# Conditioning sums over partitions in an fp32 two-block model: transposes with VectorE sums against matmuls with a column of ones

## The chip, the cores and the metric

The kernel runs on one core of one Trainium2 chip. The metric is the time of one execution on the device in microseconds, as the median of several runs.

## The reference, cut to what matters

Two blocks of two layers each work on 256 tokens of width 1024, all in fp32. The first block has a gating mixer, an attention mixer and two MLPs. The second block has four SwiGLU layers with a pooling mixer and a convolution mixer between them, and each of its six sublayers is modulated by a conditioning vector `c`:

```python
cond = jax.nn.silu(c)
for i in range(DEPTH):
    mod = (cond @ ada_w[i] + ada_b[i]).reshape(B, N_SUB, N_MOD, D_MODEL)
    shift, scale, gate = mod[:, :, 0], mod[:, :, 1], mod[:, :, 2]
    h = modulate(rms_norm(x, norm_g[i, 0]), shift[:, 0], scale[:, 0])
    x = x + 0.5 * gate[:, 0, None, :] * swiglu(h, ffn_w_in[i, 0], ffn_w_out[i, 0])
    ...
```

`ada_w` is 2 x 1024 x 9216 in fp32. What this document is about is the end of `cond @ ada_w[i]` for `shift` and `scale`.

## The kernel before

The program is written out by hand: one instruction stream for each engine, with semaphores between them. Tokens are two tiles (t = 0, 1) of 128. Weights come in slabs of 128 x 2048 through a ring of three buffers `raw`. Each product of the large layers is made of three fp32r matmuls, so a slab is split: ScalarE writes `w_hi` (L512), VectorE writes `w_lo` = raw - w_hi (L865), and TensorE multiplies w_hi with x_hi, w_lo with x_hi and w_hi with x_lo (L1327 to L1329, issued in the helper `mm`, L1315). Every tile of an up product is 12 such matmuls of 512 columns for each half of the 1024 inputs.

The phases follow one another: gate_in, positions, gate_out, mlp0, qkv, attn, attn_out, mlp1, final1, ffn0, pool, ffn1, ffn2, conv_in, conv_out, ffn3, final2. In an MLP or FFN phase, chunk c runs up products of two slabs into `up_ps`, ScalarE and VectorE make `mid` from them, TensorE turns `mid` by transposes into `tr_ps` (L1396), ScalarE and VectorE split that into hT_hi and hT_lo (L526, L876), and TensorE adds the down product to `acc`. The transposes of chunk c stand behind the down product of chunk c - 1.

`tr_ps` has two PSUM banks of 512 fp32 columns. All uses of it are numbered ("fills"); fill n goes to bank n % 2. TensorE waits in `bank(n)` (L1384) until `tr_read`, the count of fills that have been read, reaches n - 1, and raises `tr_ready` when a fill is complete.

The conditioning product runs beside the layers. VectorE multiplies pieces of `ada_w` with `cond` and adds them up over the eight groups of 128 rows in `ada_acc` (L930, L933), 128 x 9216, so that only the sum over the 128 partitions is missing. For each of the six sublayers ("sub") `modulation` makes that sum for the 16 tiles of shift and scale. On TensorE (L1487 to L1496) it is cut into two halves of eight tiles. Each tile of 128 x 128 is transposed into a quarter of a bank, so a half fills two banks and a sub four (MOD_FILLS = 4). On VectorE (L937 to L954) four sums over the free axis (L944) read 128 x 512 each and write `mod_sum`; then come the add of the bias (L949), the gain (L951) and `mod_ready`.

The places are fixed by the order of the code. In mlp1, the two halves of sub 0 stand behind the two token tiles of the second up slab of chunk 1 (`between`, L1519). In ffn0, ffn1 and ffn2, the halves of the first sub stand inside the up product of chunk 1, one up tile apart (L1657 to L1659). In ffn0 and ffn2 there is a second sub: its half 0 stands ahead of the first down slab and its half 1 behind it, right ahead of the transposes of mid of chunk 1 (L1641 to L1650). On VectorE, `modulation` stands ahead of the ada pieces of chunk 1 in mlp1, ahead of a split for the first sub of an FFN (L1176), and behind the next split for the second (L1184).

The gates, the third part of each sub, are summed over partitions in another way already: two matmuls (L1622) with `ones[:, :]`, 128 x 128, as the weights and 512 columns of `ada_acc` streamed.

Of the kernel before, what the change touches and what calls it, by code (L numbers as in the profile page):

```python
# [17 lines left out]
ALU = mybir.AluOpType  # L18
ACT = mybir.ActivationFunctionType
AX_X = mybir.AxisListType.X  # L20
# [3 lines left out]
P = 128  # L24
D = 1024
KT = D // P
# [7 lines left out]
FILL = 4  # L34
# [34 lines left out]


MODS = {"mlp1": (0,), "ffn0": (1, 2), "ffn1": (3,), "ffn2": (4, 5)}
MOD_FILLS = 2 * KT // FILL
GATES = {"ffn0": (0, 1), "ffn1": (2,), "ffn2": (3, 4), "ffn3": (5,)}
GATE_HALF = {sub: n for subs in GATES.values() for n, sub in enumerate(subs)}
FFN_AT = {"ffn0": 0, "ffn1": 1, "ffn2": 2, "ffn3": 3}
# [84 lines left out]
def build(nc, x, mix_norm_g, mlp_norm_g, final_norm_g, a_w_in, a_ln_g, a_ln_b, a_w_s, a_b_s, a_w_out,  # L160
# [7 lines left out]
    with ctx:  # L168
        def sb(name, shape, dt=F32):
            return ctx.enter_context(nc.sbuf_tensor(name, shape, dt))  # L170
# [9 lines left out]
        ada_acc = sb("ada_acc", [P, ADA_COLS])  # L180
# [9 lines left out]
        ident = flip[:, 1, :]  # L190
        ones = sb("ones", [P, P])
# [4 lines left out]
        msq = sb("msq", [P, TT])  # L196
        rstd = sb("rstd", [P, TT])
        neg_half = sb("neg_half", [P, 1])
        mod_sum = sb("mod_sum", [P, 2 * KT])
        mod = sb("mod", [P, 3, 2 * KT])  # L200
        gain = sb("gain", [P, 3, KT])
        den = sb("den", [P, 2 * HEADS])
# [37 lines left out]
        tr_ps = ctx.enter_context(nc.psum_tensor("tr_ps", [P, 2, 512], F32))  # L240
# [14 lines left out]
        tr_ready, tr_hi, tr_read = sem("tr_ready"), sem("tr_hi"), sem("tr_read")  # L255
# [585 lines left out]
        def _(dve):  # L841
            steps = [0]

            def own(ins):

                ins.then_inc(dve_step, 1)
                steps[0] += 1
                dve.wait_ge(dve_step, steps[0])
# [88 lines left out]
            def modulation(name, sub):  # L937


                layer, s = divmod(sub, 3)  # L940
                fill = mid_fill(at[name], name, 0) + TT + MOD_FILLS * MODS[name].index(sub)
                for q in range(MOD_FILLS):
                    dve.wait_ge(tr_ready, fill + q + 1)
                    nc.vector.tensor_reduce(mod_sum[:, q * FILL:(q + 1) * FILL],  # L944
                                            tr_ps[:, (fill + q) % 2, :].rearrange("p (f n) -> p f n", n=P),
                                            AX_X, ALU.add).then_inc(tr_read, 1)
                dve.wait_ge(tr_read, fill + MOD_FILLS)
                b = adabT[:, layer, s * 3 * KT:s * 3 * KT + 2 * KT]
                own(nc.vector.tensor_tensor(mod[:, s, :], mod_sum[:, :], b, ALU.add))  # L949
                r0 = ROWS["norm"][0] + KT * sub  # L950
                nc.vector.scalar_tensor_tensor(out=gain[:, s, :], in0=mod[:, s, KT:2 * KT], scalar=1.0,  # L951
                                               in1=vecT[:, r0:r0 + KT], op0=ALU.add, op1=ALU.mult)\
                    .then_inc(mod_ready, 1)
                dve.wait_ge(mod_ready, sub + 1)  # L954
# [19 lines left out]
            last = lambda name: at[name].slab - 1  # L974
# [13 lines left out]
            for c in range(4):  # L988
                ahead(g)
                if c == 1:  # L990
                    p = at["positions"]
# [37 lines left out]
            p = at["gate_out"]  # L1029
            for n in range(NORM_FILLS):  # L1030
                t, b = divmod(n, KT // FILL)
# [43 lines left out]
            p = at["qkv"]  # L1075
# [53 lines left out]
            p = at["attn_out"]  # L1129
# [98 lines left out]
            for q in range(POOLS):  # L1228
                dve.wait_ge(tr_read, at["pool"].tr + q + 1)
                k = slice(2 * q, 2 * q + 2)  # L1230
                for f in range(2):
                    n = 2 * q + f
# [13 lines left out]
            p = at["conv_in"]  # L1246
            own(nc.vector.memset(uT[:, :, 0:CONV_W - 1], 0.0))
            g = p.slab
            q = at["conv_out"]
# [60 lines left out]
        def _(pe):  # L1310
# [3 lines left out]
            def mm(dst, a, b, start=False, stop=False):  # L1314
                return nc.tensor.matmul(dst, a, b, start=start, stop=stop, skip_group_check=True)  # L1315
# [68 lines left out]
            def bank(tr, i=None, per=0):  # L1384

                if tr >= 2:
                    pe.wait_ge(tr_read, plus(i, tr - 1, per))
                return tr_ps[:, tr % 2, :]
# [62 lines left out]
            for c in range(1, 4):  # L1451
                up_chunk(g + 2 * c, free=(gelu_done, 2 * (c - 1) + 1, 0))
                if c == 1:
                    p = at["positions"]
# [7 lines left out]
                    for n in range(NG):  # L1462
                        c0 = n * VLEN
                        while c0 < (n + 1) * VLEN:
                            c1 = min((n + 1) * VLEN, (c0 // 512 + 1) * 512)
                            last = mm(acc[0:HEADS, c0 // D, c0 % D:c0 % D + c1 - c0], rel[:, n * HEADS:(n + 1) * HEADS],
                                      mask_sb[:, n, c0 - n * VLEN:c1 - n * VLEN], start=True, stop=True)
# [4 lines left out]
            for t in range(TT):  # L1472
                pe.wait_ge(vn_ready, t + 1)
                for q in range(GROUPS):
                    last = mm(acc[:, t, q * P:(q + 1) * P], ws_T[:, q, :], g_v[:, t, q * P:(q + 1) * P],
                              start=True, stop=True)
                last.then_inc(mix_ready, 1)
            p = at["gate_out"]
            for n in range(NORM_FILLS):
                t, b = divmod(n, KT // FILL)  # L1480
# [6 lines left out]
            def modulation(name, sub, half):  # L1487

                fill = mid_fill(at[name], name, 0) + TT + MOD_FILLS * MODS[name].index(sub)
                pe.wait_ge(ada_step, 8 * ((sub // 3) * ADA_UNITS + 6 * (sub % 3) + 4))  # L1490
                for q in range(half * MOD_FILLS // 2, (half + 1) * MOD_FILLS // 2):
                    dst = bank(fill + q)
                    for f in range(FILL):
                        n = (sub % 3) * 3 * KT + q * FILL + f
                        last = nc.tensor.transpose(dst[:, f * P:(f + 1) * P], ada_acc[:, n * P:(n + 1) * P], ident)  # L1495
                    last.then_inc(tr_ready, 1)  # L1496

            def mlp(name):
# [35 lines left out]
            p = at["qkv"]  # L1534
# [23 lines left out]
            p = at["attn"]  # L1558
# [49 lines left out]
            p = at["attn_out"]  # L1608
# [74 lines left out]
            p = at["pool"]  # L1683

            pe.wait_ge(pool_landed, 16)
            for q in range(POOLS):
                dst = up_ps[:, q // 2, (q % 2) * TOKENS:(q % 2 + 1) * TOKENS]
# [6 lines left out]
            for q in range(POOLS):  # L1694
                dst = bank(p.tr + q)
# [72 lines left out]
```

## Time and profile before

| | before |
|---|---|
| median of 3 runs | 1605.37 us (1604.02 to 1610.68) |
| the profiled execution | 1607.08 us, span 1605.3 us |
| PE matmul busy | 1524.8 us (95%), 7069 instructions |
| PE weight load busy | 1254.0 us (78%) |
| VectorE busy | 1038.2 us (65%), 1110 instructions |
| ScalarE busy | 707.9 us (44%) |
| DMA | 345.83 MB, mean 215 GB/s |
| mean granted TensorE clock | 0.981 |

The profile counts an engine as busy when an instruction is running on it; matmuls are pipelined, so PE (TensorE matmul) being busy doesn't mean that it runs at its peak. PEld is the weight load, which overlaps PE. In a timeline, the duration of a matmul contains its latency; what a stream of matmuls costs is read from the distance of their starts.

### The profile page before, as it was taken

The page shows a single profiled execution, that of the slowest core. Times are in us where ns is not written, and L with a number is a line of the kernel's source. Part 1 is how long each engine was busy: PE and PEld are TensorE (multiplying, and loading weights), DVE is VectorE, ACT ScalarE, POOL GpSimd, SP SyncE. Part 2 cuts the span into 40 slices and gives each one's busy share as a digit, 9 for nine tenths or more (in the row PEclk, how much of TensorE's full clock was granted, in tenths as well). Part 3 has the DMA queues.
Part 4 walks back from the last instruction along what each step waited for, and adds up shares of the span by engine and source line. Part 5 has one row for each costly group of instructions (what it writes and reads, how often), then busy time and mean ns, then how long its engine had stood idle before and what let it go on. Part 6 is the DMA issues. An engine that isn't in the chain of part 4 may idle for free.

```text
span 1605.3 us, 20507 instructions
## 1 busy us (share of the span) xinstructions
PE 1524.8 (95%) x7069; PEld 1254.0 (78%) x7069; DVE 1038.2 (65%) x1110; ACT 707.9 (44%) x831; POOL 22.0 (1%) x63
## 2 busy tenths in 40 slices
PE   5899999999999999799998899998999999999997
PEld 4778888788778888678887788886788878778886
DVE  4748777545548767567887778887645464764444
ACT  5345444543545454444443434444344444454442
POOL 1000000000000000000000000000000000000000
PEclk9999999999999999899999899999999999999999
DMA  8438777557508788558896279886455546445552
GB/s 260 174 126 324 270 269 274 159 173 243 175 12 295 282 287 289 188 183 309 302 311 229 85 256 318 303 313 217 144 184 188 189 140 204 143 158 185 190 190 76
DMA packets 201892, 345.83 MB, mean 215 GB/s; under 512 B 9531, under 2 KB 105027, under 8 KB 201836
## 3 DMA queue, kind: packets, MB, share of 16 engines
q1 hardware_dynamic: 161420, 267.22, 49.5%
q10 hardware_dynamic: 40416, 77.86, 13.9%
q8 instruction: 35, 0.57, 0.1%
q14 instruction: 21, 0.17, 0.0%
HBM read 343.96 MB, written 1.09 MB: 215 GB/s over the span
## 4 chain that ended last, share of the span: by engine, by line
PE 84%; DVE 8%; ACT 3%; DMA 2%; issue 2%; POOL 1%; SPq 0%; POOLq 0%; DVEq 0%; ACTq 0%
PE up_ps L1315 51%; PE acc L1315 28%; DVE w_lo L865 3%; PE tr_ps L1396 2%; DMA ada_raw<-in_ada_w 2%; PE tr_ps L1315 1%; DVE ada_acc L933 1%; ACT w_hi L512 1%; DVE res L971 1%; ACT xn L534 1%; DVE xn L968 1%; PE tr_ps L1581 1%; ACT xn L549 1%; PE tr_ps L1495 1%; POOL rstd L470 1%
## 5 line engine op out<-in xcount | busy, mean ns | idle before, releaser
L865 DVE TENSOR_TENSOR w_lo<-raw,w_hi 128x2048 fp32r<-128x2048 f32 x245 | 561.1, 2291 | 302.4 <-ACT w_hi L512 301.3
L512 ACT ACTIVATE w_hi<-raw 128x2048 fp32r<-128x2048 f32 x245 | 469.5, 1916 | 313.1 <-PE up_ps L1315 256.7
L1315 PE MATMUL up_ps<-w_hi,xT_hi 128*128 128x512 f32 x1264 | 506.0, 400 | 22.8 <-DVE xT_lo L887 16.5
L1315 PE MATMUL up_ps<-w_hi,xT_lo 128*128 128x512 f32 x1264 | 497.5, 394 | 0.0
L1315 PE MATMUL up_ps<-w_lo,xT_hi 128*128 128x512 f32 x1264 | 497.1, 393 | 0.0
L1315 PEld LDWEIGHTS up_ps<-w_hi,xT_hi 128*128 128x128 f32 x1264 | 240.4, 190 | 75.3 <-issue 16.9
L1315 PEld LDWEIGHTS up_ps<-w_hi,xT_lo 128*128 128x128 f32 x1264 | 240.1, 190 | 51.4
L1315 PEld LDWEIGHTS up_ps<-w_lo,xT_hi 128*128 128x128 f32 x1264 | 240.8, 190 | 47.6
L933 DVE SCALAR_TENSOR_TENSOR ada_acc<-ada_raw,cond,ada_acc 128x512 f32 (+1 forms) x252 | 189.3, 751 | 15.7 <-DMA ada_raw<-in_ada_w 8.0
L1315 PE MATMUL acc<-w_hi,hT_hi 128*128 128x512 f32 x624 | 194.3, 393 | 4.8 <-DVE hT_lo L876 4.8
L1315 PE MATMUL acc<-w_hi,hT_lo 128*128 128x512 f32 x624 | 193.0, 391 | 0.0
L1315 PE MATMUL acc<-w_lo,hT_hi 128*128 128x512 f32 x624 | 192.9, 391 | 0.0
L1315 PEld LDWEIGHTS acc<-w_hi,hT_hi 128*128 128x128 f32 x624 | 116.5, 188 | 30.1 <-DVE hT_lo L876 4.0
L526 ACT ACTIVATE hT_hi<-tr_ps 128x256 fp32r<-128x256 f32 (+1 forms) x122 | 47.8, 441 | 207.4 <-PE tr_ps L1396 203.6
L1315 PEld LDWEIGHTS acc<-w_lo,hT_hi 128*128 128x128 f32 x624 | 117.7, 189 | 24.6
L1315 PEld LDWEIGHTS acc<-w_hi,hT_lo 128*128 128x128 f32 x624 | 117.5, 188 | 24.5
L876 DVE TENSOR_TENSOR hT_lo<-tr_ps,hT_hi 128x256 fp32r<-128x256 f32 (+1 forms) x122 | 55.4, 494 | 75.7 <-ACT hT_hi L526 75.4
L752 ACT ACTIVATE pre<-up_ps 128x256 f32<-128x256 f32 x88 | 33.9, 385 | 134.4 <-PE up_ps L1315 134.3
L534 ACT ACTIVATE xn<-res 128x1024 f32<-128x1024 f32 x24 | 25.7, 1072 | 78.6 <-DVE res L971 70.0
L1167 DVE TENSOR_TENSOR mid<-pre,up_ps 128x256 f32<-128x256 f32 x88 | 34.9, 416 | 22.8 <-ACT pre L752 22.8
L1396 PE MATMUL tr_ps<-flip,xn 128*128 128x128 f32 x160 | 26.4, 318 | 20.1 <-DVE xn L880 15.9
L1396 PEld LDWEIGHTS tr_ps<-flip,mid 128*128 128x128 f32 x304 | 36.6, 140 | 11.2 <-issue 4.2
(121 smaller groups left out, 788.6 us busy)
## 6 DMA issues: line engine op xcount, KB each, us to landing
raw<-in_ffn_w_in SPq DMA_DIRECT2D x176, 512.0 KB, 4.7
ada_raw<-in_ada_w ACTq DMA_DIRECT2D x72, 1024.0 KB, 6.9
raw<-in_ffn_w_out SPq DMA_DIRECT2D x88, 512.0 KB, 4.4
raw<-in_w_up SPq DMA_DIRECT2D x64, 512.0 KB, 4.7
raw<-in_w_down SPq DMA_DIRECT2D x64, 512.0 KB, 4.6
raw<-in_b_w_qkv SPq DMA_DIRECT2D x36, 512.0 KB, 4.4
raw<-in_conv_w_in SPq DMA_DIRECT2D x24, 512.0 KB, 4.6
raw<-in_a_w_in SPq DMA_DIRECT2D x16, 512.0 KB, 6.3
```

Source lines behind the costliest of these rows:

```text
L470: nc.gpsimd.tensor_tensor(dst, src, neg_half[:, 0:1], ALU.pow).then_inc(ready, 1)
L512: nc.scalar.activation(w_hi[:, slot, :], raw[:, slot, :], ACT.Copy).then_inc(hi_ready, 1)
L526: nc.scalar.activation(dst, src, ACT.Copy).then_inc(tr_hi, 1)
L534: nc.scalar.activation(xn[:, t, :], res[:, t, :], ACT.Square, accum_out=sumsq[:, t:t + 1]).then_inc(sumsq_ready[t], 1)
L549: a = nc.scalar.activation(dst, src, ACT.Identity, bias=bias, scale=scale)
L752: nc.scalar.activation(pre[:, t, 0:HALF], up_ps[:, t, 0:HALF], ACT.Silu).then_inc(silu_done, 1)
L865: nc.vector.tensor_tensor(w_lo[:, slot, :], raw[:, slot, :], w_hi[:, slot, :].bitcast(F32), ALU.subtract).then_inc(lo_ready, 1)
L876: nc.vector.tensor_tensor(lo, src, hi.bitcast(F32), ALU.subtract).then_inc(tr_read, 1)
L933: a = nc.vector.scalar_tensor_tensor(out=dst, in0=src, scalar=cond[:, k:k + 1], in1=dst, op0=ALU.mult, op1=ALU.add)
L1167: nc.vector.tensor_tensor(mid[:, t, 0:HALF], pre[:, t, 0:HALF], up_ps[:, t, HALF:UPN], ALU.mult).then_inc(ffn_mid, 1)
L1315: return nc.tensor.matmul(dst, a, b, start=start, stop=stop, skip_group_check=True)
L1396: last = nc.tensor.transpose(dst[:, q * P:(q + 1) * P], tile, ident)
```

## The change

The sum over the partitions is made by TensorE itself. Each 128 x 128 tile of `ada_acc` is the weight operand of a matmul whose other operand is one column of `ones`, and the result is one column of a bank. The 16 tiles of a sub go to 16 columns of one bank, so a sub has one fill (MOD_FILLS = 1). The semaphore is raised once, behind the second half. VectorE has no sums and no `mod_sum` any more; its bias add reads the bank.

```diff
-MOD_FILLS = 2 * KT // FILL
+MOD_FILLS = 1
...
-        mod_sum = sb("mod_sum", [P, 2 * KT])
...
                 fill = mid_fill(at[name], name, 0) + TT + MOD_FILLS * MODS[name].index(sub)
-                for q in range(MOD_FILLS):
-                    dve.wait_ge(tr_ready, fill + q + 1)
-                    nc.vector.tensor_reduce(mod_sum[:, q * FILL:(q + 1) * FILL],
-                                            tr_ps[:, (fill + q) % 2, :].rearrange("p (f n) -> p f n", n=P),
-                                            AX_X, ALU.add).then_inc(tr_read, 1)
-                dve.wait_ge(tr_read, fill + MOD_FILLS)
                 b = adabT[:, layer, s * 3 * KT:s * 3 * KT + 2 * KT]
-                own(nc.vector.tensor_tensor(mod[:, s, :], mod_sum[:, :], b, ALU.add))
+                dve.wait_ge(tr_ready, fill + 1)
+                nc.vector.tensor_tensor(mod[:, s, :], tr_ps[:, fill % 2, 0:2 * KT], b, ALU.add).then_inc(tr_read, 1)
+                dve.wait_ge(tr_read, fill + 1)
...
                 fill = mid_fill(at[name], name, 0) + TT + MOD_FILLS * MODS[name].index(sub)
                 pe.wait_ge(ada_step, 8 * ((sub // 3) * ADA_UNITS + 6 * (sub % 3) + 4))
-                for q in range(half * MOD_FILLS // 2, (half + 1) * MOD_FILLS // 2):
-                    dst = bank(fill + q)
-                    for f in range(FILL):
-                        n = (sub % 3) * 3 * KT + q * FILL + f
-                        last = nc.tensor.transpose(dst[:, f * P:(f + 1) * P], ada_acc[:, n * P:(n + 1) * P], ident)
+                dst = bank(fill)
+                for f in range(half * KT, (half + 1) * KT):
+                    n = (sub % 3) * 3 * KT + f
+                    last = mm(dst[:, f:f + 1], ada_acc[:, n * P:(n + 1) * P], ones[:, 0:1], start=True, stop=True)
+                if half:
                     last.then_inc(tr_ready, 1)
```

TensorE in mlp1, from the last up matmuls of token tile 1 of chunk 1 into half 1 of sub 0 and the first down slab, before (`flip` holds the identity, and the names in brackets are semaphores that the instruction waits for):

```order
L1315 MATMUL up_ps<-w_hi,xT_lo 128x512
L1495 MATMUL tr_ps<-flip,ada_acc 128x128 [waits tr_read,ada_step]
L1495 MATMUL tr_ps<-flip,ada_acc 128x128 x3
L1495 MATMUL tr_ps<-flip,ada_acc 128x128 [waits tr_read]
L1495 MATMUL tr_ps<-flip,ada_acc 128x128 x3
L1315 MATMUL acc<-w_hi,hT_hi 128x512 [waits tr_read,lo_ready]
```

and now (the helper `mm` is L1310 in the changed file):

```order
L1310 MATMUL up_ps<-w_hi,xT_lo 128x512
L1310 MATMUL tr_ps<-ones,ada_acc 128x1 [waits tr_read,ada_step]
L1310 MATMUL tr_ps<-ones,ada_acc 128x1 x7
L1310 MATMUL acc<-w_hi,hT_hi 128x512 [waits tr_read,lo_ready]
```

Eight transposes have become eight matmuls with one column of output, and the second wait for `tr_read` is gone.

VectorE in ffn0, from the gates through chunk 1, before:

```order
L1149 TENSOR_TENSOR region<-acc,region 128x1024 x2
L1154 TENSOR_TENSOR region<-region 128x1024
L944 TENSOR_REDUCE mod_sum<-tr_ps 128x4 x4
L949 TENSOR_TENSOR mod<-mod_sum,adabT 128x16
L951 SCALAR_TENSOR_TENSOR gain<-mod,vecT 128x8
L865 TENSOR_TENSOR w_lo<-raw,w_hi 128x2048
L1167 TENSOR_TENSOR mid<-pre,up_ps 128x256 x2
L865 TENSOR_TENSOR w_lo<-raw,w_hi 128x2048
L944 TENSOR_REDUCE mod_sum<-tr_ps 128x4 x4
L949 TENSOR_TENSOR mod<-mod_sum,adabT 128x16
L951 SCALAR_TENSOR_TENSOR gain<-mod,vecT 128x8
L876 TENSOR_TENSOR hT_lo<-tr_ps,hT_hi 128x2x128 x2
```

and now:

```order
L1144 TENSOR_TENSOR region<-acc,region 128x1024 x2
L1149 TENSOR_TENSOR region<-region 128x1024
L943 TENSOR_TENSOR mod<-tr_ps,adabT 128x16
L946 SCALAR_TENSOR_TENSOR gain<-mod,vecT 128x8
L864 TENSOR_TENSOR w_lo<-raw,w_hi 128x2048
L1162 TENSOR_TENSOR mid<-pre,up_ps 128x256 x2
L864 TENSOR_TENSOR w_lo<-raw,w_hi 128x2048
L943 TENSOR_TENSOR mod<-tr_ps,adabT 128x16
L946 SCALAR_TENSOR_TENSOR gain<-mod,vecT 128x8
L875 TENSOR_TENSOR hT_lo<-tr_ps,hT_hi 128x2x128 x2
```

The four sums ahead of each bias add are gone, the add reads `tr_ps`, and the order of the rest is as it was.

## Rows read from the trace of the kernel before

**Rows 1.** The page: busy us, share of the span and instructions; the chain that ended last.

```profile
PE 1524.8 (95%) x7069; PEld 1254.0 (78%) x7069; DVE 1038.2 (65%) x1110; ACT 707.9 (44%) x831; POOL 22.0 (1%) x63
...
PE 84%; DVE 8%; ACT 3%; DMA 2%; issue 2%; POOL 1%; SPq 0%; POOLq 0%; DVEq 0%; ACTq 0%
```

**Rows 2.** Groups by line and shape: busy us, mean ns | idle before, releasers.

```profile
L1495 PE MATMUL tr_ps<-flip,ada_acc 128*128 128x128 f32 x96 | 12.7, 274 | 1.7 <-DVE mod_sum L944 1.7
L944 DVE TENSOR_REDUCE mod_sum<-tr_ps 128x4 f32<-128x512 f32 x24 | 15.4, 684 | 4.2 <-PE tr_ps L1495 4.2
L949 DVE TENSOR_TENSOR mod<-mod_sum,adabT 128x16 f32<-128x16 f32 x6 | 1.1, 175 | 0.2
```

**Rows 3.** Timeline of PE, mlp1, half 0: start us, us, what.

```profile
497.89 0.39 PE L1315 MATMUL up_ps<-w_lo,xT_hi 128*128 128x512 f32 x1
498.12 0.39 PE L1315 MATMUL up_ps<-w_hi,xT_lo 128*128 128x512 f32 x1
...
499.46 0.40 PE L1315 MATMUL up_ps<-w_lo,xT_hi 128*128 128x512 f32 x1
```

**Rows 4.** Timeline of PE, mlp1, half 1.

```profile
501.74 0.39 PE L1315 MATMUL up_ps<-w_hi,xT_lo 128*128 128x512 f32 x1
503.21 1.16 PE L1495 MATMUL tr_ps<-flip,ada_acc 128*128 128x128 f32 x8 [1.09 <-DVE mod_sum L944]
504.13 0.70 PE L1315 MATMUL acc<-w_hi,hT_hi 128*128 128x512 f32 x2
504.67 0.63 PE L1315 MATMUL acc<-w_lo,hT_hi 128*128 128x512 f32 x2
```

**Rows 5.** Timeline of PE, ffn2, half 1 of its first sub.

```profile
1128.36 0.39 PE L1315 MATMUL up_ps<-w_hi,xT_lo 128*128 128x512 f32 x1
...
1130.63 0.39 PE L1315 MATMUL up_ps<-w_lo,xT_hi 128*128 128x512 f32 x1
```

**Rows 6.** Timeline of PE, ffn0, half 1 of its second sub.

```profile
713.76 0.62 PE L1315 MATMUL acc<-w_hi,hT_lo 128*128 128x512 f32 x2
...
715.69 0.41 PE L1396 MATMUL tr_ps<-flip,mid 128*128 128x128 f32 x2 [0.44 <-DVE mod_sum L944]
716.29 0.41 PE L1396 MATMUL tr_ps<-flip,mid 128*128 128x128 f32 x2 [0.19 <-DVE mod_sum L944]
...
716.93 0.40 PE L1315 MATMUL up_ps<-w_lo,xT_hi 128*128 128x512 f32 x1
```

**Rows 7.** Group of the gate matmuls, twelve in the program.

```profile
L1315 PE MATMUL acc<-ada_acc,ones 128*128 128x512 f32 x24 | 10.9, 592 | 0.0
```

**Rows 8.** Timeline of PE: gate matmuls of ffn0; full fp32 matmuls of qkv.

```profile
693.99 3.60 PE L1315 MATMUL acc<-ada_acc,ones 128*128 128x512 f32 x8
...
334.76 2.02 PE L1315 MATMUL tr_ps<-flip,xn 128*128 128x128 f32 x16
336.54 0.48 PE L1315 MATMUL up_ps<-w_hi,xT_hi 128*128 128x512 f32 x1
```

**Rows 9.** Groups of fp32 weight loads of 8 and of 128 columns.

```profile
L1315 PEld LDWEIGHTS acc<-region 33*8 33x8 f32 x10 | 0.8, 86 | 1.2 <-issue 0.5
L1315 PEld LDWEIGHTS tr_ps<-flip,mid 128*128 128x128 f32 x32 | 3.9, 192 | 0.2
```

**Rows 10.** Timeline of DVE, ffn0.

```profile
706.61 2.29 DVE L865 TENSOR_TENSOR w_lo<-raw,w_hi 128x2048 fp32r<-128x2048 f32 x1
...
714.85 1.29 DVE L944 TENSOR_REDUCE mod_sum<-tr_ps 128x4 f32<-128x512 f32 x2 [1.06 <-PE tr_ps L1495]
```

**Rows 11.** Stretches: length, busy us of PE, PEld, DVE, ACT, POOL (instructions), PEclk, DMA share, GB/s.

```profile
650.80:654.20 3.40, 1.54 (x12) 1.17 (x11) 3.40 (x4) 2.40 (x3) 0.00 (x0) 1.00 0.53 170
654.30:657.60 3.30, 3.30 (x9) 2.55 (x9) 2.60 (x2) 0.38 (x1) 0.00 (x0) 0.50 0.88 283
...
1377.90:1381.30 3.40, 2.35 (x15) 1.25 (x14) 2.99 (x8) 1.45 (x3) 0.00 (x0) 1.00 1.00 353
1381.30:1384.70 3.40, 3.40 (x17) 2.83 (x17) 2.33 (x5) 2.77 (x3) 0.00 (x0) 1.00 0.45 152
```

## The prediction

> **What bounds the kernel now.** I read the page first [rows 1]. TensorE (PE) is busy 1524.8 of 1605.3 us, and the chain of work that ended last runs through it for 84% of the span: a microsecond added to PE in a stretch where it never waits is a microsecond on the end. Next, the groups by line [rows 2]: the 96 transposes of the conditioning sums are 12.7 us of PE, the 24 VectorE (DVE) sums behind them 15.4 us. PE waited 1.7 us for those sums inside the transposes, and again at the transposes of mid in two places [rows 6]; DVE waited 4.2 us for PE. Little can therefore be won by freeing DVE.
>
> Then the timeline, to price one half of a modulation (eight tiles) as PE feels it. The streaming matmuls around it start every 0.227 us (497.89, 498.12 in [rows 3]). In [rows 3] the last of them starts at 498.12 and the second one after the transposes at 499.46; that is 1.34 us, less two steps of 0.227, so a half costs 0.88 us. Eight of the twelve halves cost this (0.88 or 0.89). Four cost more. In mlp1, half 1 [rows 4]: from 501.74 to 504.67, less three steps (the row at 504.13 holds two), is 2.25 us, 1.09 of it a wait for mod_sum, since a third bank isn't free until a sum has read it. In ffn2, half 1 of its first sub [rows 5]: from 1128.36 to 1130.63 less two steps is 1.82. In ffn0, the second half of the second sub with the four transposes of mid behind it [rows 6]: PE goes from 713.99 (second matmul of the pair at 713.76) to 716.93, less two steps, 2.50 us, of which 0.44 and 0.19 are waits for mod_sum; ffn2 has the same again, 2.52. All twelve: 8 x 0.883 + 2.25 + 1.82 + 2.50 + 2.52 = **16.15 us**, with eight transposes of mid inside.
>
> **The change part by part.** *The new matmuls.* They are full fp32 matmuls, not transposes. The gate product has two instructions for each of six subs, twelve, but the trace has 24 of them [rows 7]: a full fp32 matmul runs as two pairs of load and matmul. A transpose runs as one (96 written, 96 recorded). So a half goes from 8 pairs to 16. One pair of the new kind (128 weight columns loaded, one column streamed) isn't in the trace. Its bounds: below, the pace follows the streamed columns. Gate matmuls of 512 columns are (3.60-0.59)/7 = 0.43 us apart, the sixteen of 128 columns in qkv 0.111 us [rows 8] (from 334.76 to 336.54 in 16); the line through both gives 0.005 us at one column. Above, each load is paid in full before the next, 0.192 us, the duration of one 128-column fp32 load [rows 9]. I take 0.111 us. The duration of a load depends on its columns: 8 columns take 86 ns, 128 take 192 [rows 9], so 120 columns cost 106 ns and 128 occupy the load path for about 113 ns. The stream of sixteen in [rows 8] carries such a load every 0.111 us, its loads overlapping (0.192 long, 0.111 apart), and one streamed column cannot shorten a load. So a plain half becomes 16 x 0.111 = 1.78 us, 0.90 more than before.
>
> A page sets another price. The Trainium skill's page "TensorE: Matmul & The Clock Gate", section "Back-to-back issue gap", gives a matmul of 1 to 64 columns about 60 cycles (25 ns); by that alone a half would be an estimated 0.4 us and the change a gain. Its section "LDWEIGHTS" ties the load to its columns instead, which is what [rows 9] shows. The first reading is rival D below.
>
> *Waits that go.* Both halves write one bank, so the wait inside a half (mlp1, ffn2) goes. The first half needs the same bank free as before.
>
> *Waits that come or stay.* In ffn0 and ffn2 the second transposes of mid now need the bank of the sums: the last matmul ends about 0.17 us after its start (a 128-column transpose takes 0.273 us [rows 2], some 0.107 of it its columns), DVE takes 0.175 us for its add [rows 2], and from a DVE end to PE's restart the trace has 0.16 us (a sum ends at 714.85 + 0.684, PE starts at 715.69; [rows 2, 6, 10]). The first two transposes fill 0.22 of that; about 0.2 is left as a wait and 0.15 as the slow restart, 0.35 in all. These two halves with their four transposes become 1.78 + 0.44 + 0.35 = 2.57 us.
>
> *Sum.* 10 x 1.78 + 2 x 2.57 = 22.9 us against 16.15: **+6.8 us**, all on PE.
>
> *DVE.* It loses 24 sums of 0.684 us and six adds change only their source. It was waiting for PE at each, so that is worth nothing. Instead it starts the add only after the whole second half. In ffn0 the add and gain end about 1.0 us later, and behind them stands the w_lo split of 706.61 [rows 10], then the product mid. The split is for chunk 2, whose second matmul starts at 716.93 [rows 6]: 2.29 us of work with over 7 us of cover. If the cover were gone, PE would lose the 1.0 us. The mid product moves with PE itself. ScalarE, SyncE and POOL queues keep their instructions; what they wait for on PE moves by the same 1 to 2 us a site, and raw slots are released with it.
>
> *Gates, transposes of the norms, the loops.* Not touched. In mlp1 and ffn1 the number of bank fills before what follows changes from four to one, which swaps banks 0 and 1 for the later fills, at no cost.
>
> The profiled execution has 1607.08 us (span 1605.3), 1.7 above the median of the runs, inside their spread. 1607.08 + 6.8 = 1613.9; from the median, 1605.37 + 6.8 = **1612.2 us**, +0.42%. A measurement of this kernel tells about 0.5%, 8.0 us, from no change: the forecast is within it, but not by much.
>
> **The rivals.**
>
> *B, the clock (slower).* A burst of one-column matmuls leaves the array almost without streamed columns for 1.8 us, twelve times. The granted clock has two levels, and in this trace it fell after thin stretches [rows 11]: after 650.8 to 654.2, where PE was busy 1.54 of 3.4 us (eight transposes, then a wait), it was 0.50 for 3.3 us, 1.2 GHz, PE then did 9 matmuls instead of the 14 to 15 that a step of 0.227 allows, some 1.3 us lost; 3.4 us at half clock lose 1.7. Against it: after 1377.9 to 1381.3 (2.35 busy, transposes only) it stayed at 1.00 [rows 11], and streaming matmuls stand on both sides of most bursts. Likeliest places are the last halves of ffn0 and ffn2, where burst, transposes and wait make 2.6 us. The decisive point is one fall: 6.8 + 1.7 = 8.5 us is over 0.5%. Two falls make 1615.6, four 1619, and a fall that lasts twice as long costs 3.4. The same page says, in "PE-mode transpose", that transposes don't count as busy for the gate; by that the old bursts would be as thin as the new and B would lose its ground. The trace disagrees: sixteen transposes with hardly anything else left the clock at 1.00 [rows 11].
>
> *C, loads unhidden (slower).* A one-column matmul gives the next load nothing to hide under; at 0.192 us a pair each half adds 16 x 0.081 = 1.3 us, 15.6 in twelve: 1627.8. Against: loads already overlap one another in [rows 8].
>
> *D, columns set the pace (faster).* If the loads ran ahead of the matmuls without limit, a half would cost 0.1 us, the sum 12 x 0.1 + 2 x 0.79 = 2.8 against 16.15: 1592.0. Against: the load's own 113 ns.
>
> *E, the change buys fewer instructions than I count.* If a one-column matmul were issued as one pair, a half stays at 8 x 0.111 = 0.89, and only the waits go: 10 x 0.89 + 2 x (0.89 + 0.79) = 12.3, or 3.9 less: 1601.5, no measurable change. Against: 24 records for twelve gate instructions [rows 7].
>
> **How the numbers follow.** Forecast A 0.55, B 0.27, C 0.08, D 0.04, E 0.06. Of A some 0.08 ends above 8 us (a pair at 0.118 does it). Slower 0.08 + 0.27 + 0.08 = 0.43; within 0.5% 0.47 + 0.06 = 0.53; faster 0.04. The range goes from 1603 (A with cheap restarts and a low run; E and D left out) to 1621 (B with up to five falls); above lies C and a little of B.
>
> **What would show it.** In the profile after: 192 matmuls and 192 loads onto tr_ps from ada_acc, 0.11 us apart; no wait of PE for DVE inside a half; six adds from tr_ps of about 0.18 us, each preceded by a DVE wait of 1 to 2 us; a wait of 0.2 us for the add in ffn0 and ffn2; the twelve halves taking 22.9 us; granted clock 1.00 around 500, 700 to 717, 926 to 932 and 1125 to 1142. A pace of 0.19, 96 records, or a clock of 0.50 just after a burst would each name the rival that won. A PE wait for w_lo in chunk 2 would show the cover of the later DVE work to be too thin.

## The result and the profile after

| | before | after |
|---|---|---|
| median | 1605.47 us (6 runs, 1603.21 to 1610.68) | 1613.61 us (6 runs, 1612.08 to 1617.94) |
| ratio to before, 95% interval | | 1.0051 (1.0034 to 1.0068) |
| span of the profiled execution | 1605.3 us | 1613.0 us |
| PE busy | 1524.8 us, 7069 | 1536.1 us, 7165 |
| VectorE busy | 1038.2 us, 1110 | 1023.1 us, 1086 |
| mean granted clock | 0.981 | 0.982 |

The change costs 8.1 us by the medians, 7.7 by the profiled spans. The groups by line that answer to [rows 2] and to the load of [rows 9]:

```profile
L1310 PEld LDWEIGHTS tr_ps<-ones,ada_acc 128*128 128x128 f32 x192 | 23.3, 191 | 0.9
L1310 PE MATMUL tr_ps<-ones,ada_acc 128*128 128x1 f32 x192 | 22.1, 245 | 0.0
L943 DVE TENSOR_TENSOR mod<-tr_ps,adabT 128x16 f32<-128x16 f32 x6 | 1.0, 174 | 22.4 <-PE tr_ps L1310 22.4
```

192 records stand for 96 written matmuls. VectorE now waits 22.4 us for TensorE in six waits; it has time to spare and gives none of it to the end. The timeline of PE and DVE in mlp1, half 1, which answers to [rows 4]:

```profile
504.57 0.39 PE L1310 MATMUL up_ps<-w_hi,xT_lo 128*128 128x512 f32 x1
504.57 1.98 PEld L1310 LDWEIGHTS tr_ps<-ones,ada_acc 128*128 128x128 f32 x16
...
504.80 1.84 PE L1310 MATMUL tr_ps<-ones,ada_acc 128*128 128x1 f32 x16
...
506.50 0.72 PE L1310 MATMUL acc<-w_hi,hT_hi 128*128 128x512 f32 x2
506.67 0.17 DVE L943 TENSOR_TENSOR mod<-tr_ps,adabT 128x16 f32<-128x16 f32 x1 [2.33 <-PE tr_ps L1310]
...
507.06 0.63 PE L1310 MATMUL acc<-w_lo,hT_hi 128*128 128x512 f32 x2
```

The wait of 1.09 us is gone. From 504.57 to 507.06 less three steps of 0.227 is 1.81 us, where the same place took 2.25. The price of a half now is best seen in ffn2, half 1 of its first sub, with the matmuls on both sides:

```profile
1134.35 0.39 PE L1310 MATMUL up_ps<-w_hi,xT_lo 128*128 128x512 f32 x1
1134.58 1.84 PE L1310 MATMUL tr_ps<-ones,ada_acc 128*128 128x1 f32 x16
1136.28 0.49 PE L1310 MATMUL up_ps<-w_hi,xT_hi 128*128 128x512 f32 x1
1136.60 0.40 PE L1310 MATMUL up_ps<-w_lo,xT_hi 128*128 128x512 f32 x1
```

1136.60 - 1134.35 - 0.454 = 1.80 us; the same place before, 1.82 [rows 5], was the one with a wait of 0.65:

```profile
1129.40 1.16 PE L1495 MATMUL tr_ps<-flip,ada_acc 128*128 128x128 f32 x8 [0.65 <-DVE mod_sum L944]
```

Counted in this way, the ten plain halves take 1.80 each and the two before the transposes of mid 2.62, together 23.2 us against 16.15: **+7.1 of the 7.7 us of span**. The other 0.6 is the balance of differences elsewhere, of which one is large: behind the transposes ahead of conv_out the clock fell in this profile and not in the one before. From the last up matmul ahead of them to the sixtieth record of TensorE behind it, the change takes 15.97 us and the kernel before 14.69. Both kernels do the same work there, so I count the 1.3 us as scatter of the clock. The other places give back 0.7, not traced one by one.

```profile
1383.00:1386.40 3.40, 1.81 (x11) 0.87 (x9) 2.25 (x5) 1.23 (x2) 0.00 (x0) 1.00 1.01 347
1386.40:1389.80 3.40, 3.21 (x11) 2.43 (x12) 3.40 (x8) 1.83 (x4) 0.00 (x0) 0.51 0.79 259
```

The granted clock behind a burst stays up:

```profile
506.60:510.00 3.40, 3.40 (x16) 2.79 (x16) 3.15 (x7) 1.46 (x1) 0.00 (x0) 1.00 0.96 367
720.90:724.30 3.40, 3.40 (x16) 2.83 (x16) 1.89 (x3) 2.22 (x3) 0.00 (x0) 1.00 0.49 155
```

### The profile page after: what moved, and what is told of

It is laid out like the page before. It is cut to its first block, busy times and chain, and to the rows that moved or that the text cites. A ratio compares the mean times of both kernels' runs of the same rounds, so it can differ in the third digit from the quotient of the medians.

```text
span 1613.0 us, 20675 instructions
## 1 busy us (share of the span) xinstructions
PE 1536.1 (95%) x7165; PEld 1266.2 (78%) x7165; DVE 1023.1 (63%) x1086; ACT 708.1 (44%) x831; POOL 22.1 (1%) x63
## 3 DMA queue, kind: packets, MB, share of 16 engines
HBM read 343.96 MB, written 1.09 MB: 214 GB/s over the span
## 4 chain that ended last, share of the span: by engine, by line
PE 85%; DVE 6%; ACT 3%; issue 2%; DMA 2%; POOL 1%; SPq 0%; POOLq 0%; DVEq 0%; ACTq 0%
PE up_ps L1310 52%; PE acc L1310 28%; DVE w_lo L864 2%; PE tr_ps L1391 2%; PE tr_ps L1310 2%; DMA ada_raw<-in_ada_w 1%; ACT xn L533 1%; DVE ada_acc L932 1%; ACT xn L548 1%; ACT w_hi L511 1%; DVE res L966 1%; PE tr_ps L1576 1%; DVE xn L963 1%; POOL rstd L469 1%; DMA raw<-in_a_w_in 0%
## 5 line engine op out<-in xcount | busy, mean ns | idle before, releaser
L1310 PE MATMUL up_ps<-w_hi,xT_hi 128*128 128x512 f32 x1264 | 505.9, 400 | 22.7 <-DVE xT_lo L886 16.4
L1310 PE MATMUL up_ps<-w_hi,xT_lo 128*128 128x512 f32 x1264 | 496.8, 393 | 0.0
L1310 PE MATMUL up_ps<-w_lo,xT_hi 128*128 128x512 f32 x1264 | 496.7, 393 | 0.0
L1310 PEld LDWEIGHTS up_ps<-w_hi,xT_hi 128*128 128x128 f32 x1264 | 240.2, 190 | 75.7 <-issue 16.8
L1310 PEld LDWEIGHTS up_ps<-w_hi,xT_lo 128*128 128x128 f32 x1264 | 240.0, 190 | 51.8
L1310 PEld LDWEIGHTS up_ps<-w_lo,xT_hi 128*128 128x128 f32 x1264 | 240.7, 190 | 47.9
L1310 PE MATMUL acc<-w_hi,hT_hi 128*128 128x512 f32 x624 | 193.4, 391 | 5.0 <-DVE hT_lo L875 5.0
L1310 PE MATMUL acc<-w_hi,hT_lo 128*128 128x512 f32 x624 | 192.4, 389 | 0.0
L1310 PE MATMUL acc<-w_lo,hT_hi 128*128 128x512 f32 x624 | 192.3, 389 | 0.0
L1310 PEld LDWEIGHTS acc<-w_hi,hT_hi 128*128 128x128 f32 x624 | 116.1, 188 | 30.2 <-DVE hT_lo L875 4.2
L1310 PEld LDWEIGHTS acc<-w_hi,hT_lo 128*128 128x128 f32 x624 | 117.1, 188 | 24.5
L1310 PEld LDWEIGHTS acc<-w_lo,hT_hi 128*128 128x128 f32 x624 | 117.1, 188 | 24.5
L1391 PE MATMUL tr_ps<-flip,xn 128*128 128x128 f32 x160 | 25.6, 312 | 18.9 <-DVE xn L879 14.4
```

Source lines behind the costliest of these rows:

```text
L1391: last = nc.tensor.transpose(dst[:, q * P:(q + 1) * P], tile, ident)
```

## Experiments

Below, "cost of the halves" is always the sum of twelve differences read as above: from the last streaming matmul ahead of a half to the second behind it, less two steps of 0.227 us. The change stands at 23.2 us and 1613.6 us. Medians of the kernel before, measured on the same chips, were 1606.2, 1607.5 and 1607.95 in the three sets (e1 to e4; e5 to e8; e9 to e12); ratios are to those. The change itself was measured once, beside a median of 1605.47, so a difference to its 1613.6 also carries the step from set to set, up to 2.5 us; the ratios don't.

One step of the attention phase moves single times by several us: behind it the clock stayed low for 6.8 us in eleven of the fourteen profiles and for 17.1 us in three (e1, e2, e3). In e1, the wide32 kernel, it was 0.50 until 431 us, in the change's profile only until about 421:

```profile
421.00:431.00 10.00, 10.00 (x39) 8.40 (x39) 2.06 (x8) 2.87 (x7) 0.00 (x0) 0.50 0.43 144
```

The same stretch of the change's profile, with 73 matmuls for 39:

```profile
421.00:431.00 10.00, 10.00 (x73) 8.56 (x72) 4.22 (x15) 4.42 (x11) 0.00 (x0) 1.00 0.55 179
```

So I read mechanisms from the cost of the halves and the total from the ratios.

### Does the streamed column set the pace?

```diff
-                    last = mm(dst[:, f:f + 1], ada_acc[:, n * P:(n + 1) * P], ones[:, 0:1], start=True, stop=True)
+                    last = mm(dst[:, 32 * f:32 * (f + 1)], ada_acc[:, n * P:(n + 1) * P], ones[:, 0:32],
+                              start=True, stop=True)
```

> Each conditioning matmul streams 32 columns of ones instead of one (32 columns of the bank per tile, the add reads every 32nd); weight loads and counts as in the change. Load theory (a pair costs what its 128-column load costs, 0.111 us): the columns are under the load, pairs stay 0.111 us apart, the twelve halves stay at 23.2 us together and the time at 1613.6, within 1 us. Rival, streamed columns set the pace on top of the load: 192 x 31 more columns at 0.0008 us make +5 us, 1618. Clock theory: nothing changes, it stayed at 1.00 already.

Measured: 1617.72 us, ratio 1.0059 (1.0036 to 1.0081), an interval that overlaps the change's. The halves cost 23.2 us, as with one column. 32 times the columns are free: the streamed columns don't set the pace. The expected time, 1613.6 within 1 us, was missed by 4 us, which are not in the halves. The profiled span is 7.7 us longer than the change's; the 10.3 us more at half clock in the attention phase make some 5 of that.

### Does the load set it?

Two loads of 64 columns for each tile, with the outputs on the lower and the upper 64 partitions (e2), the same with all outputs on the lower 64 (e9, which leaves out half of the sums), and four loads of 32 (e10):

```diff
-                    last = mm(dst[:, f:f + 1], ada_acc[:, n * P:(n + 1) * P], ones[:, 0:1], start=True, stop=True)
+                    for r in range(0, P, P // 2):
+                        last = mm(dst[r:r + P // 2, f:f + 1], ada_acc[:, n * P + r:n * P + r + P // 2], ones[:, 0:1],
+                                  start=True, stop=True)
```

In e9 the second output of each tile goes to the same partitions, one column further:

```diff
+                        last = mm(dst[0:P // 2, 2 * f + r // 64:2 * f + r // 64 + 1],
+                                  ada_acc[:, n * P + r:n * P + r + P // 2], ones[:, 0:1], start=True, stop=True)
```

> Each 128x128 tile is taken as two weight loads of 64 columns, with its two outputs on partitions 0 to 63 and 64 to 127: 384 pairs instead of 192, the same number of weight columns. Load theory (cost goes with weight columns): pairs 0.056 us apart, a half stays near 1.8 us, the time within 2 us of the change's 1613.6. Rival, each pair has a fixed price whatever its columns (0.111 us): a half takes 3.6 us, +1.78 x 12 = +21.3 us, 1635. Between the two, a floor per pair shows as its distance.

> As e2_half_loads (two weight loads of 64 columns a tile), but both write partitions 0 to 63 (in two columns), so that all pairs use the same 64 array columns; the sums of partitions 64 to 127 are left out and the conditioning is wrong. e2 took 1.23 us a half, 0.038 us a pair, under the 0.056 that half a load costs. If loads to different array columns overlap: here 0.056 us a pair, 1.8 us a half. If e2's gain is that a 64-column load is cheaper than half a 128-column one: 1.23 us again. If a pair has a fixed price in one group: up to 3.6 us.

> Each tile as four weight loads of 32 columns, its outputs on four groups of 32 partitions: 64 pairs a half, same result. If loads to different array columns overlap fully: under 1.2 us a half. If each pair has a floor of about 0.025 us or more (e2's 0.038 may be near it): 64 x 0.025 to 64 x 0.038 = 1.6 to 2.4 us, no better than e2, time 1609 to 1617.

The timeline of PE in mlp1, half 0, for e2, e9 and e10:

```profile
505.38 1.10 PE L1310 MATMUL tr_ps<-ones,ada_acc 128*64 128x1 f32 x32
506.41 0.50 PE L1310 MATMUL up_ps<-w_hi,xT_hi 128*128 128x512 f32 x1
```

```profile
500.72 2.03 PE L1310 MATMUL tr_ps<-ones,ada_acc 128*64 128x1 f32 x32
502.67 0.50 PE L1310 MATMUL up_ps<-w_hi,xT_hi 128*128 128x512 f32 x1
```

```profile
500.90 0.71 PE L1310 MATMUL tr_ps<-ones,ada_acc 128*32 128x1 f32 x64
501.54 0.50 PE L1310 MATMUL up_ps<-w_hi,xT_hi 128*128 128x512 f32 x1
```

| kernel | pairs a half | us from pair to pair | a half, us | twelve halves, us | median, ratio |
|---|---|---|---|---|---|
| the change | 16 | 1.70/16 = 0.106 | 1.80 | 23.2 | 1613.6, 1.0051 |
| e9, 64 columns, one group | 32 | 1.95/32 = 0.061 | 2.16 | 27.5 | 1627.0, one run |
| e2, 64 columns, two groups | 32 | 1.03/32 = 0.032 | 1.23 | 16.2 | 1609.3, 1.0010 (0.9994 to 1.0026) |
| e10, 32 columns, four groups | 64 | 0.64/64 = 0.010 | 0.84 | 11.6 | 1607.8, 0.9993 (0.9975 to 1.0011) |

The loads in e2, e9 and e10, by group (columns as above: busy us, mean ns):

```profile
L1310 PEld LDWEIGHTS tr_ps<-ones,ada_acc 128*64 128x64 f32 x384 | 12.2, 138 | 4.2 <-issue 3.9 <-DVE ada_acc L932 0.4
```

```profile
L1310 PEld LDWEIGHTS tr_ps<-ones,ada_acc 128*64 128x64 f32 x384 | 23.3, 138 | 4.2 <-issue 4.2
```

```profile
L1310 PEld LDWEIGHTS tr_ps<-ones,ada_acc 128*32 128x32 f32 x768 | 7.5, 110 | 4.2 <-issue 4.2
```

A load takes 191, 138 and 110 ns at 128, 64 and 32 columns: 53 ns for 64 columns, 28 for 32, 0.83 to 0.88 ns each. Within one group of array columns (the columns behind the output partitions) the distance follows that: half the columns, 0.061 for 0.106 us. These are burst lengths divided by pairs; inside a burst, once it runs, the starts are 0.112 and 0.058 us apart. A fixed price per pair would have left it at 0.106. So the load sets the pace; that is shown. What I hadn't expected is the second line of the comparison: loads of the same size that alternate between different groups of array columns overlap. e2 and e9 issue the same 32 loads of 64 columns and differ only in where the outputs go, 1.03 against 1.95 us; the 384 loads are 138 ns long in both, but cover 12.2 us in e2 and 23.3 in e9. The starts in e2 are 6 and 52 ns apart in turn, together the 58 of one pair in e9: each group takes its next load at its own pace, and the groups run side by side. In e10 four starts, one in each group, take 32 ns. With four groups the sixteen tiles-and-passes of a half take 0.64 us, a good third of the change's 1.70, and by the halves the whole product costs 4.6 us less than the transposes did. The medians don't show that: e10 is at 0.9993, and its interval ends at 4.0 us under the kernel before, just short of it.

Of the expectations, e2's load theory (1.8 us a half, the time within 2 us of 1613.6) was too slow by 0.57 us and 4.3 us, since it had no overlap; e9's 1.8 us a half came out at 2.16, and e10's half under 1.2 us was met.

### What a longer burst does to the clock

```diff
-                    last = mm(dst[:, f:f + 1], ada_acc[:, n * P:(n + 1) * P], ones[:, 0:1], start=True, stop=True)
+                    for _ in range(2):
+                        last = mm(dst[:, f:f + 1], ada_acc[:, n * P:(n + 1) * P], ones[:, 0:1], start=True, stop=True)
```

> Every conditioning matmul is issued twice in a row (384 pairs of 128 weight columns), result unchanged. Load theory: 192 more pairs at 0.111 us, +21.3 us on TensorE, none of it hidden, 1634.9 and a half of 3.6 us. Clock theory: bursts of 3.6 us with nearly no streamed columns let the granted clock fall behind several of twelve; each fall of 3.4 us costs 1.7, so 1640 to 1655 and PEclk 0.50 rows behind the bursts. Rival, part of the burst was hidden in waits: less than +21.

Measured: 1662.01 us, ratio 1.0346 (1.0327 to 1.0365), 48.4 us over the change. The first half takes 3.59 us (505.08 to 508.57 for its 32 pairs), as priced; twelve times 1.79 more are 21.5. The rest is the clock: it was low for 119.0 us in this profile and for 61.4 in the change's, and 57.6 us more at half pace are 28.8, of which some 5 belong to the attention phase. That is about what is left of the 48.4. The stretches behind the first two bursts:

```profile
509.90:513.20 3.30, 3.30 (x11) 2.64 (x9) 0.00 (x0) 0.06 (x1) 0.00 (x0) 0.51 0.79 266
516.90:520.20 3.30, 3.30 (x9) 2.55 (x9) 3.16 (x6) 0.00 (x0) 0.00 (x0) 0.54 0.40 155
```

9 to 11 matmuls at 1.2 GHz where 15 fit at 2.4. At eleven of the twelve bursts the clock fell like this, behind the burst or, at later ones, inside it: 51 us at 0.50 in all. In e9, whose bursts are 1.95 us of pairs, it is there already, behind five of twelve:

```profile
937.10:939.30 2.20, 2.20 (x34) 2.14 (x34) 0.09 (x1) 0.38 (x1) 0.00 (x0) 1.00 0.00 0
939.90:943.30 3.40, 3.40 (x9) 2.62 (x9) 2.34 (x2) 0.00 (x0) 0.00 (x0) 0.54 0.02 4
```

So rival B is a real mechanism. In the profiles of the change, e1 and e6, with 1.70 us of pairs a burst, none of the falls comes within 6 us behind a burst. e9 is a single execution, and its bursts differ from the change's in two things, 0.25 us of length and loads of 64 columns; which of them brings the falls isn't separated. PE busy is 2.20 of 2.20 in the first of these rows: a burst of loads looks fully busy and still lets the clock fall.

### What the removed waits and VectorE's time are worth

Four VectorE sums of 128x512 (0.62 us each here) put back into the change, once between the wait for the matmuls and the add (e5), once ahead of that wait (e6); and the kernel before with a copy of four columns in place of each sum, which leaves the sums out (e4).

```diff
                 dve.wait_ge(tr_ready, fill + 1)
+                for q in range(4):
+                    nc.vector.tensor_reduce(mod_sum[:, q * FILL:(q + 1) * FILL],
+                                            res[:, 0, 0:512].rearrange("p (f n) -> p f n", n=P), AX_X, ALU.add)
                 nc.vector.tensor_tensor(mod[:, s, :], tr_ps[:, fill % 2, 0:2 * KT], b, ALU.add).then_inc(tr_read, 1)
```

> The change, with four VectorE sums of 128x512 (over res, into a scratch tile) put back between the wait for the matmuls and the bias add, so that VectorE has the work of before and releases the bank later. Theory (VectorE's time counts only where TensorE needs the bank): at 0.6 to 0.7 us a sum the second transposes of mid in ffn0 and ffn2 wait 2.4 to 2.7 us more each, +5 us, 1618.5; nothing at the other four subs, since the splits behind them have over 4 us of cover. Rival, VectorE's work counts everywhere: +2.6 x 6 = +16 us, 1629.

> The same four sums, but ahead of the wait for the matmuls, in VectorE's own idle time there (22.4 us in six waits, 3.7 us each). Theory: nothing, 1613.6 within 1 us. Rival (taking 24 sums off VectorE was worth something by itself in the change): up to +5 us or more.

> The kernel before with its transposes, but VectorE copies 4 columns of each bank instead of summing 512, which leaves out the conditioning sums. This frees VectorE of 24 x 0.5 us but keeps the four fills. If the waits that the change removed came from the length of the sums: PE's 3.0 us of waits for mod_sum shrink to under 1 us, time 1602.5 to 1603.5. If they came from VectorE standing in earlier work (a split until 502.46 us in mlp1) and from the number of fills: about 0.5 us goes at each of four places, 1.8 us in all, 1603.6. If VectorE time counts by itself (12 us less busy): up to 1593.

e5: 1623.05 us (only 4 runs, 1619 to 1628), ratio 1.0104 (1.0073 to 1.0136); the halves cost 28.5 us, 5.3 more than the change. All of it is at the two places that the theory named; ffn0, PE and DVE:

```profile
717.86 0.42 PE L1395 MATMUL tr_ps<-flip,mid 128*128 128x128 f32 x2
718.04 2.46 DVE L945 TENSOR_REDUCE mod_sum<-res 128x4 f32<-128x512 f32 x4 [3.92 <-PE tr_ps L1314]
720.42 0.16 DVE L947 TENSOR_TENSOR mod<-tr_ps,adabT 128x16 f32<-128x16 f32 x1
...
720.73 0.66 PE L1395 MATMUL tr_ps<-flip,mid 128*128 128x128 f32 x2 [2.45 <-DVE mod L947]
721.04 0.79 PE L1314 MATMUL up_ps<-w_hi,xT_hi 128*128 128x512 f32 x1
```

The other ten halves keep 1.80. Behind both longer waits the clock fell in the profile (from 721.04 to the next start at 721.63 it is 0.59 us, where 0.33 is usual). The median is some 4 us over what the halves say, and the falls don't explain that: the profiled run has them and took 1619.4 us, near the expected 1618.5. The four times are 1619.1, 1619.4, 1626.7 and 1627.8; what makes the upper two isn't shown.

e6: 1611.94 us, ratio 1.0031 (1.0017 to 1.0045), 1.7 us under the change where 1 was allowed; halves 23.2. VectorE's 15 us of sums are worth nothing when they lie in its own waits; with or without them the kernel is the same within the measurement.

e4: 1604.75 us, ratio 0.9994 (0.9982 to 1.0007); halves 13.7, 2.5 us less than before. In mlp1 a wait of 0.56 us stays, because VectorE is in a split until about 502.5; the waits in front of the transposes of mid are gone (0.63 to 0.08 in ffn0). The 3 us of waits thus came mostly from the length of the sums and partly from VectorE's queue, between the first two of the three expectations. The 2.5 us are 0.16%, inside the interval of the ratio, so the time neither shows nor denies them. Freeing VectorE by itself gave nothing beyond these waits.

### Is the two-pass matmul the loss?

`ada_acc` kept as fp32r and multiplied with two fp32r columns, one pass. The accumulations are rounded to fp32r, so this computes the conditioning less precisely.

```diff
-                    last = mm(dst[:, f:f + 1], ada_acc[:, n * P:(n + 1) * P], ones[:, 0:1], start=True, stop=True)
+                    last = mm(dst[:, 2 * f:2 * f + 2], ada_r[:, n * P:(n + 1) * P], one_r[:, 0:2], start=True, stop=True)
```

> The change with ada_acc kept as fp32r (each accumulation is rounded to it) and multiplied in one pass with two fp32r columns: 96 pairs instead of 192; the precision of the conditioning sums is reduced. If the two-pass form of a full fp32 matmul is the whole loss: a half takes 8 x 0.111 = 0.9 us, 12 x 0.9 = 10.8 us less than the change, 1602.8, below the kernel before by about 2.7 us, the waits that went. Rival (the burst has a fixed part, or clock): a smaller gain, 1605 or more. If an fp32r load takes as long as two fp32 ones: no change.

1604.53 us, ratio 0.9983 (0.9965 to 1.0002), 9.1 us under the change, 10.9 by the two ratios; halves 12.5 us, 10.7 less. The ten times lie in two groups of five, 1600.2 to 1600.9 and 1608.1 to 1609.3, and the median between them, so the halves are the firmer number. A plain half takes 0.91 us, what eight transposes took (0.88): the load count is what the change doubled. The load lasts as long as an fp32 one:

```profile
L1316 PEld LDWEIGHTS tr_ps<-one_r,ada_acc 128*128 128x128 f32 x96 | 12.5, 191 | 0.9
```

### Into TensorE's own waits

The first sub of mlp1, ffn0, ffn1 and ffn2 moved to the start of the phase: half 0 ahead of the first transposes of xn, half 1 behind them, into `up_ps` of token tile 1, which is free there. Four of six subs leave the chunk loop.

```diff
             def first_chunk(name):
...
+                if name in EARLY:
+                    early(name, 0)
                 turn_norm(name, 0)
+                if name in EARLY:
+                    early(name, 1)
                 for t in range(TT):
+                    if t and name in EARLY:
+                        pe.wait_ge(mod_ready, EARLY[name] + 1)
```

> The change, with both halves of the first sub of mlp1, ffn0, ffn1 and ffn2 moved to the start of the phase: half 0 ahead of the first transposes of xn, half 1 behind them, into a free bank of up_ps. TensorE idles there in the profile of the change: 1.19 us behind in mlp1; 2.23 ahead and 1.40 behind in ffn0; 2.14 and 1.18 in ffn1; 1.46 and 2.05 in ffn2. Theory (a pair costs only where TensorE has no wait to put it in): 10.6 of the 14.4 us are hidden, 1603.0, faster than the kernel before. Rival: the granted clock is 0.50 there and loads run at half pace (3.6 us a half), hiding only 6 to 7 us: 1607 or more; or, the other way, TensorE busy there keeps the clock up and gives 3 to 5 us more: 1599.

> e8_moved and e2_half_loads together: 64-column loads, and the first sub of four phases in TensorE's idle time at their start. e8 was 7.5 us under the change and e2 4.3; four halves stay in the open at 1.23 instead of 1.80 (-2.3 us), and of those moved what didn't fit into the wait shrinks by up to 0.6 us each. Expected 1602 to 1604, 0.2 to 0.4% under the kernel before. Rival: the clock, which was lower in e8 for 66 us in all, takes it back: 1606.

> As e11 with 32-column loads. If e10's half is under 1.2 us: 0 to 2 us under e11. If pairs have a floor: 0 to 5 us over it.

| kernel | median (runs) | ratio to before |
|---|---|---|
| e8, moved, 128-column loads | 1606.06 (10) | 0.9991 (0.9977 to 1.0005) |
| e11, moved, 64-column loads | 1600.39 (12) | 0.9960 (0.9945 to 0.9976) |
| e12, moved, 32-column loads | 1596.11 (6) | 0.9933 (0.9911 to 0.9955) |

e8's median missed its 1603.0 and lies near the clock rival's 1607, but its profiled run took 1601.76 us. In that run, at the entry of ffn0, the second half ran at half clock, sixteen pairs in 3.41 us instead of 1.84:

```profile
669.01 1.97 PE L1398 MATMUL tr_ps<-flip,xn 128*128 128x128 f32 x8 [0.56 <-DVE xn L881]
670.77 3.41 PE L1317 MATMUL up_ps<-ones,ada_acc 128*128 128x1 f32 x16
674.04 0.77 PE L1317 MATMUL up_ps<-w_hi,xT_hi 128*128 128x512 f32 x1
```

Its wait for the norm is only 0.56 us long there, where the change waited 2.25. From the last streaming matmul ahead of this entry to the first behind it is 7.66 us, in the change 5.13. Later waits take that back: to the 96th streaming matmul behind the entry it is 38.14 us, in the change 43.42 with two halves of 1.80 inside, so e8 is 1.7 us ahead once they are taken off. Counted in the same way it loses 3.2 us in mlp1, where the clock fell for 6.8 us at the moved halves and not in the change, 1.7 in ffn1 and 0.1 in ffn2. So the profiled run hides 11.1 of the 14.4 us, about what the theory said (10.6). Half-pace loads are real, but why the median lies 4 us above that run isn't shown.

In e12 the entry of ffn0:

```profile
663.90 0.71 PE L1317 MATMUL up_ps<-ones,ada_acc 128*32 128x1 f32 x64
666.21 1.09 PE L1398 MATMUL tr_ps<-flip,xn 128*128 128x128 f32 x8 [1.60 <-DVE xn L881]
667.24 0.71 PE L1317 MATMUL up_ps<-ones,ada_acc 128*32 128x1 f32 x64
668.71 0.47 PE L1317 MATMUL up_ps<-w_hi,xT_hi 128*128 128x512 f32 x1 [0.76 <-DVE xT_lo L888]
```

Waits remain on both sides, so both halves are free here. From the last streaming matmul ahead of the entry to the first behind it, mlp1, ffn0, ffn1 and ffn2 take 3.21, 5.12, 30.01 and 4.99 us, in the change 2.46, 5.13, 30.21 and 4.99: the moved halves are free but for 0.75 us in mlp1. Counted to the 96th streaming matmul, as above, it is 1.5 us in all, since in ffn1 the second half and what follows it run at half clock. The four halves left in the chunks cost 4.9 us. 16.15 - 4.9 - 1.5 = 9.7 us under the kernel before is what this gives; the spans differ by 11.4 and the medians by 11.8 (interval 7.2 to 14.3). e12 is faster than both kernels, 17.5 us under the change (19 by the two ratios).

Both combinations beat their expectations: e11 came to 1600.39 where 1602 to 1604 was expected, e12 to 4.3 us under e11 where 0 to 2 was. Shorter bursts lose less when the clock is low: at the entry of ffn0 it is 6.29 us from matmul to matmul in e11 and 5.12 in e12, against 7.66 in e8. Why the times fell by more than expected isn't traced further.

## Why the prediction was right

The forecast was 1612.2 us (+6.8, within 0.5%); the median came to 1613.61, +8.1, inside the range. The ratio, 1.0051, lies just over the 0.5% that the forecast had stayed under.

- *The unit.* Pricing a half by starts of streaming matmuls, not by busy time, held: busy time would have said 22.1 - 12.7 = 9.4 us more.
- *A pair at 0.111 us.* A plain half was priced at 1.78 and takes 1.80. Inside a burst the starts are 0.112 us apart. The argument from the load's duration was right, though rows 9 compare loads that differ in rows too (33 and 128); e9, e2 and e10 show it directly at 128 rows. The two-pass count, 192 records, was right, and e7 confirms its weight. That 1.78 comes so near to 1.80 is partly luck: the second pair of a burst starts only 0.025 us behind the first, and the first streaming matmul behind a burst keeps 0.33 us to the next instead of 0.227; no term had either, and they nearly cancel.
- *Waits that go.* Both did. They offset the extra loads in mlp1 and in ffn2: 2.25 to 1.81, 1.82 to 1.80.
- *Waits that stay.* 2.57 priced, 2.62 measured; the profile calls only 0.08 us of it a wait, not 0.2, but the third transpose starts 0.35 us behind the second, where 0.11 is the usual step.
- *DVE worth nothing.* Right where VectorE waits anyway (e6, e4); e5 shows that its time does count where TensorE needs the bank. The delay of its add is covered: TensorE's waits for w_lo are 4.8 us in six, 4.9 before.
- *The size.* 22.9 forecast, 23.2 measured for the halves. The rest of the gap to 8.1 is 0.6 us of span that no term had, with the fall of the clock at the transposes of 1384 to 1388 us in it, and the scatter of the medians.
- *Rival B* at 0.27: not in the profiled run, but the mechanism and its price are real. With twice the pairs (e3) it decides. I had named the last halves of ffn0 and ffn2 as the likeliest places; the clock stood at 1.00 behind them too. One of my arguments against B was weaker than it looked: before, sixteen transposes with little else (2.35 of 3.4 us busy) left the clock at 1.00, but in the change's profile it fell within the same transposes, after a stretch of 1.81 of 3.4 us busy. The two leave it open whether transposes hold the clock up.
- *Rival C* (0.192 a pair) and *D* (columns) are refuted by the 0.106 to 0.112 us between pairs, and D again by e1. D's own price, 0.1 us a half, and the 0.4 us from the page that I named beside it are not the same reading; the measured 1.80 rules out both. *E* fell with the 192 records.
- *What the prediction didn't see*: that a load to another column group overlaps. The change has one group of 128 columns, so it changes nothing there.

The page's 25 ns for a small matmul, "TensorE: Matmul & The Clock Gate" in the Trainium skill, section "Back-to-back issue gap", isn't what a pair costs here: 0.106 us with one group, and 0.010 us with four, below it. The same section says that in a stream of loads and matmuls both set the spacing and that its short formula leaves the load out at small sizes, which fits the 0.106; the prediction passed over that. The slope of its "LDWEIGHTS" section, duration by columns, is borne out: 0.83 ns a column between 64 and 128. The recorded durations themselves are some 80 ns longer than the columns at that slope (191 ns at 128), and that part overlaps with the next load.

## What to carry over

In this kernel a matmul with one streamed column costs its weight load, and a full fp32 one costs two. Price it by weight columns, and compare with transposes by loads, not by output size: the same eight tiles cost 0.88 us as transposes, 1.80 as full fp32 matmuls, and 0.84 when each tile was split over four groups of array columns. Taking work off an engine that waits bought only the waits that others had for it (2.5 us in e4); look for the stretches where the bound engine itself waits, and put short work there.

## What the runs showed of the hardware

- Loads of 64 or 32 columns that alternate between groups of array columns overlap: the distance between pairs fell from 0.061 us (one group of 64) to 0.032 (two) and 0.010 (four groups of 32). Inside one group the next load comes after 0.112 us at 128 columns, 0.058 at 64 and 0.032 at 32.
- A full fp32 matmul is recorded as two pairs of load and matmul (192 for 96 written), an fp32 transpose as one, and an fp32r matmul of two columns as one (96 for 96).
- Streaming 32 columns instead of one behind a 128-column load costs nothing (halves 23.2 us in both).
- The clock can fall from 2.4 to 1.2 GHz behind a burst in which PE and PEld are busy all the time: at eleven of twelve bursts of 3.5 to 4.4 us (e3), behind five of twelve of 1.95 us (e9, one execution, 64-column loads), behind none of 1.70 in the change, e1 and e6. At the lower level loads take double as well (3.41 us for sixteen pairs in e8, 1.84 at the upper one).
